# Five matmul operands at other SBUF addresses: 112, 96 and 160 modulo 256 bytes instead of 128

## The chip, the cores and the metric

The kernel runs on one core of one Trainium2 chip. The metric is the device time of one execution in microseconds (us); lower is better. One execution was also profiled. In its rows PE is TensorE's matmul side, PEld its weight loads, DVE VectorE, ACT ScalarE, POOL GpSimd and SP SyncE.

## The reference: what is computed

Two transformer-like blocks are applied to 512 tokens of width 1024 (the first block also carries 16 meta tokens). All arithmetic is float32.

```python
# first block: token mixer (S5 state space + mLSTM), then a convolved, gated feed-forward
h = concatenate([meta, x])                                  # 528 x 1024
proj = rmsnorm(h, g_pre) @ w_in ; ... ; x + rmsnorm(merged @ w_out, g_post)
a = causal_dwconv(h @ w_gate, w_conv, b_conv)               # 1024 -> 2816
y = (gelu(a) * (h @ w_up)) @ w_down                         # 2816 -> 1024
# second block: 16 attention heads of three kinds, then an MLP
proj = rms_norm(x, norm_g) @ w_in                           # q, k, v, gates
y = concatenate([y_moba, y_fox, y_dil]) @ w_out ; x = x + y
x + square(relu(rms_norm(x, norm_g) @ w_up)) @ w_down       # 1024 -> 4096 -> 1024
```

## The kernel before, in words

Activations lie transposed in SBUF: features on the 128 partitions, tokens along the free axis. The weights come in "units" of 128 x 1024 floats through a ring of four buffers (`w_raw`). ScalarE rounds a unit to `w_hi` (type fp32r) and VectorE makes the rest, `w_lo`. Each activation operand is kept as such a pair too, `..._hi` and `..._lo`. A product is three matmuls, hi by hi, lo by hi and hi by lo, for each of 8 blocks of 128 input features, all into one PSUM accumulation: 24 matmuls for one unit over 512 tokens. The helper `unit` (its matmul is L1939) does this; in a row `ps<-h_lo,w_hi` the first name is the moving operand, which streams through the array, the second the stationary one, which a weight load (LDWEIGHTS, PEld) puts there. Every matmul has its own weight load.

Moving operands are 512 tokens wide, or are cut in two halves of 256 and 260 (or 264 and 264) tokens where 516 or 528 tokens have to be covered, since a PSUM bank holds 512 floats.

Everything in SBUF has a hand-made address. `at(name, shape, where)` puts a tile at byte `where` of each partition, over others that are dead by then; the base names are `HX` (byte 82560), `Zu` (151488) and `R` (170176). In this document a *phase* is the byte address at which an operand's read begins, modulo 256. The tiles that matter, with their phases as the program has them before the change:

- `h2_hi`, `h2_lo` (shown as `h_hi`, `h_lo` in rows): input of every projection of the second block, 512 wide, row stride 2048 bytes: phase 128.
- `f_hi`, `f_lo`: input of the first block's feed-forward. The view begins 4 words into rows of 576 words (2304 bytes, nine times 256). The gate units (`ffn_gate`) read halves of 256 and 260 columns from column 0: phase 112 for both. The up units (`ffn_up`) read 512 columns from column 4: phase 128.
- `ffn_hi`, `ffn_lo`: the feed-forward's activations, moving operand of its down products: phase 128.
- `mlp_hi`, `mlp_lo`: the same of the second block's MLP: phase 128.
- `y_dil_hi`, `y_dil_lo` (72 matmuls) phase 128, and `w_hi`, `w_lo`, whose 128-column blocks all begin at phase 128: not touched by the change.
- In the first block `h_hi`, `h_lo` have rows of 528 words (2112 bytes), so the phase moves by 64 from one of the 8 feature blocks to the next. Units with halves of 264 begin at 128 + 64k and 160 + 64k, which over the 8 blocks are all the multiples of 32; units with halves of 256 and 260 (read from token 12) begin at 176 + 64k, that is 176, 240, 48 and 112.

Order is by hand: each engine's program is written out, and semaphores join them. TensorE waits in `begin` for the unit's `w_lo` and for the PSUM bank to be free.

Of the kernel before, what the change touches and what calls it, by code (L numbers as in the profile page):

```python
# [25 lines left out]
KT = D_MODEL // P  # L26
SEQ, META = 512, 16
# [3 lines left out]
TW = T1 - T0  # L31
# [124 lines left out]
def build(nc, w_units, x_t, cols_in, consts_in, sel_in, ssm_b_in, ssm_c_in, alibi_in, dil_in, out):  # L156
    fp32, f32r = mybir.dt.float32, mybir.dt.float32r
# [10 lines left out]
    def region(size):  # L168
        at = place[0]
        place[0] += size  # L170
        return at

    def at(name, shape, where, dt=fp32):
        return nc.alloc_sbuf_tensor_at(name, [P] + shape, dt, offset=where)
# [6 lines left out]
    HX = place[0]  # L181
# [12 lines left out]
    Zu = region(4 * T1 * 4)  # L194
# [41 lines left out]
    yahi = at("ya_hi", [CT, T1], R + 20 * T1 * 4, f32r)  # L236
    yalo = at("ya_lo", [CT, T1], R + 24 * T1 * 4, f32r)

    fhi = at("f_hi", [KT, 576], HX + (96 - HX) % 256, f32r)[:, :, 4:4 + TW]
    flo = at("f_lo", [KT, 576], Zu + (96 - Zu) % 256, f32r)[:, :, 4:4 + TW]  # L240
    RA = R + (128 - R) % 256
    fahi = at("ffn_hi", [KT, SEQ], RA, f32r)
    falo = at("ffn_lo", [KT, SEQ], RA + 16384, f32r)
    sq0 = [at(f"first_sq{j}", [T1], Zu + 2112 * j) for j in range(4)] + [sq[0], sq[1], rows, rs]
    sqp = [at(f"tile_sq{j}", [T1], R + 2112 * j) for j in range(KT)]
    gp = [at(f"gate_pad{j}", [T1 + 2], R + 256 + 32768 + 2144 * j) for j in range(2)]
# [1 line left out]
    tup = [at(f"up{j}", [SEQ], R + 256 + 41152 + 2048 * j) for j in range(2)]  # L248
    ctmp = at("conv_tmp", [SEQ], R + 256 + 45312)

    h2hi = at("h2_hi", [KT, SEQ], HX, f32r)
    h2lo = at("h2_lo", [KT, SEQ], HX + 4 * KT * SEQ, f32r)
    V = at("v2_tok", [4, D_MODEL], R)
    sgf = at("fox_gate", [3, SEQ], R + 16384)
    qa = [at(f"q_pair{j}", [SEQ], R + 22528 + 2048 * j) for j in range(2)]
# [16 lines left out]
    wf = at("w_forget", [KT * 32], Zv + 9216)  # L272
    dilr = at("dil_mask_r", [SEQ], Zv + 1024, f32r)

    mahi = at("mlp_hi", [KT, SEQ], RA, f32r)
    malo = at("mlp_lo", [KT, SEQ], RA + 16384, f32r)
    sqm = [at(f"mlp_sq{j}", [SEQ], Z2 + 2048 * j) for j in range(KT)]
    rl = [at(f"relu{j}", [SEQ], R + 33024 + 2048 * j) for j in range(2)]
    r2 = [at(f"relu_sq{j}", [SEQ], R + 37120 + 2048 * j) for j in range(2)]
# [2410 lines left out]
```

How the kernel before makes its waits and increments, by code:

```python
    def fence(self):  # L131
        if self.last is not None:
            self.eng.wait_ge(*self.last)
# [208 lines left out]
        @block.sync  # L343
# [12 lines left out]
            def load(s, r, j):  # L356
                sp.wait_ge(lo_ready, r + (s - RING + 1))
                sp.dma_start(raw[:, j, :], w_units[bass.ds(r + s, 1), :, :].rearrange("a p c -> p (a c)")
                             if not isinstance(r, int) else w_units[r + s]).then_inc(raw_in[j], 16)
            trips = (UNITS - RING) // RING
            with sp.Fori(0, trips) as i:
                for j in range(RING):
                    load(RING + j, i * RING, j)
            for n in range(RING + trips * RING, UNITS):
                load(n, 0, n % RING)
            for m in range(KT - 1):
                sp.wait_ge(sem("out_ready"), m + 1)
                sp.dma_start(out[:, m * SEQ:(m + 1) * SEQ], ot[m % 2][:, :]).then_inc(sem(f"out_done{m % 2}"), 16)
            for hf in range(2):
                sp.wait_ge(sem("out_ready"), KT + hf)
                c0 = hf * SEQ // 2
                sp.dma_start(out[:, (KT - 1) * SEQ + c0:(KT - 1) * SEQ + c0 + SEQ // 2], ot[1][:, c0:c0 + SEQ // 2]
                             ).then_inc(sem("out_done1"), 16)
            sp.wait_ge(sem("out_done0"), 16 * KT // 2)
            sp.wait_ge(sem("out_done1"), 16 * (KT // 2 + 1))
# [16 lines left out]
            def post_square(norm, m, src):  # L394
                if m == 0:
                    act.wait_ge(sem("rs_ready"), norm)
                elif m >= 3:
```

## Time and profile before

| | |
|---|---|
| median of 3 runs | 1450.04 us (1449.85 to 1450.05) |
| the profiled execution's own time | 1451.67 us |
| its span, first to last instruction | 1449.9 us |
| TensorE matmul busy | 98% of the span, 9151 matmuls |
| granted TensorE clock | 0.999 of full speed |

The profiled execution's time is 1.8 us above its span and 1.6 us above the median. A matmul's record in the timeline has a start and a length; matmuls overlap, so the length says little about throughput. The distance from one start to the next, here called the *pitch*, is what a matmul costs in a running stream.

### The profile page before, as it was taken

How to read it: one execution, taken by the hardware profiler on the slowest of the kernel's cores; microseconds unless marked ns; L12 is line 12 of the kernel's file. 1: busy time of each engine (PE TensorE's matmuls, PEld its weight loads, DVE VectorE, ACT ScalarE, POOL GpSimd, SP SyncE). 2: the span in 40 equal slices, each digit the busy share in tenths (PEclk: the TensorE clock that was granted, in tenths of full speed). 3: DMA queues.
4: the chain of work that ended last, by engine and by line, in shares of the span. 5: the costliest groups of instructions: out<-in, count | busy, mean ns of one | idle time of the engine just before them, and what ended most of it. 6: DMA issues, size and time to landing. Idle time of an engine off the chain costs nothing.

```text
span 1449.9 us, 23195 instructions
## 1 busy us (share of the span) xinstructions
PE 1425.1 (98%) x9151; PEld 1229.5 (85%) x9151; DVE 844.1 (58%) x1267; ACT 606.9 (42%) x924; POOL 305.1 (21%) x287
## 2 busy tenths in 40 slices
PE   8999999999999999999999999999999999999999
PEld 7999999999998988998998777767678888888887
DVE  6888554457465543554355637898877534344355
ACT  6552577643343321222124445666645314233230
POOL 2660333300115621560364000002103000000000
PEclk9999999999999999999999999999999999999999
DMA  5212111223312322323233132101133323323321
GB/s 206 74 60 76 58 59 66 67 86 138 109 64 73 102 101 88 101 87 101 88 102 126 64 104 73 59 29 59 44 117 117 102 88 102 102 87 103 100 93 68
DMA packets 35846, 128.30 MB, mean 88 GB/s; under 512 B 4084, under 2 KB 4468, under 8 KB 35632
## 3 DMA queue, kind: packets, MB, share of 16 engines
q1 hardware_dynamic: 34608, 122.18, 25.5%
q10 hardware_dynamic: 864, 4.33, 0.8%
q8 instruction: 63, 1.03, 0.3%
q0 software_dynamic: 288, 0.57, 0.1%
q14 instruction: 23, 0.19, 0.0%
HBM read 124.92 MB, written 2.10 MB: 88 GB/s over the span
## 4 chain that ended last, share of the span: by engine, by line
PE 70%; DVE 11%; ACT 8%; POOL 7%; issue 2%; DMA 0%; ACTq 0%; DVEq 0%; SPq 0%; POOLq 0%
PE ps L1939 59%; PE ps L2345 3%; DVE w_lo L967 2%; POOL gate_conv L1757 2%; POOL conv_tmp L1860 2%; ACT w_hi L392 2%; DVE rot L971 2%; POOL phase_tmp L1757 1%; PE ps L2464 1%; PE ps L2441 1%; PE ps L2403 1%; ACT conv_tap L516 1%; DVE rot L1223 1%; POOL gate_conv L1857 1%; PE ps L2454 1%
## 5 line engine op out<-in xcount | busy, mean ns | idle before, releaser
L967 DVE TENSOR_TENSOR w_lo<-w_raw,w_hi 128x1024 fp32r<-128x1024 f32 (+2 forms) x225 | 294.1, 1309 | 168.1 <-ACT w_hi L392 167.1
L1939 PE MATMUL ps<-h_hi,w_hi 128*128 128x512 f32 (+3 forms) x1168 | 332.6, 334 | 5.1 <-DMA consts<-consts 2.2
L1939 PE MATMUL ps<-h_hi,w_lo 128*128 128x512 f32 (+3 forms) x1168 | 321.7, 325 | 0.0
L1939 PE MATMUL ps<-h_lo,w_hi 128*128 128x512 f32 (+3 forms) x1168 | 321.6, 324 | 0.0
L392 ACT ACTIVATE w_hi<-w_raw 128x1024 fp32r<-128x1024 f32 (+2 forms) x226 | 231.0, 1032 | 171.8 <-PE ps L1939 166.2
L1939 PEld LDWEIGHTS ps<-h_hi,w_hi 128*128 128x128 f32 x1168 | 196.8, 189 | 34.4 <-issue 11.7
L1939 PEld LDWEIGHTS ps<-h_lo,w_hi 128*128 128x128 f32 x1168 | 196.7, 189 | 19.7 <-issue 2.9
L1939 PEld LDWEIGHTS ps<-h_hi,w_lo 128*128 128x128 f32 x1168 | 196.4, 189 | 17.9
L1939 PE MATMUL ps<-f_hi,w_hi 128*128 128x256 f32 (+1 forms) x488 | 129.6, 319 | 0.0
L1939 PE MATMUL ps<-f_hi,w_lo 128*128 128x256 f32 (+1 forms) x488 | 129.6, 319 | 0.0
L1939 PE MATMUL ps<-f_lo,w_hi 128*128 128x256 f32 (+1 forms) x488 | 129.5, 319 | 0.0
L1939 PE MATMUL ps<-mlp_lo,w_hi 128*128 128x512 f32 (+1 forms) x264 | 101.1, 383 | 0.0
L1939 PE MATMUL ps<-mlp_hi,w_hi 128*128 128x512 f32 (+1 forms) x264 | 101.1, 383 | 0.0
L1939 PE MATMUL ps<-mlp_hi,w_lo 128*128 128x512 f32 (+1 forms) x264 | 101.1, 383 | 0.0
L1939 PEld LDWEIGHTS ps<-f_hi,w_hi 128*128 128x128 f32 x488 | 82.3, 188 | 7.9 <-DVE w_lo L967 0.4
L971 DVE TENSOR_TENSOR y_sum<-y_sum,ps 128x512 f32<-128x512 f32 (+2 forms) x40 | 27.0, 674 | 105.4 <-PE ps L1939 105.4
L1939 PEld LDWEIGHTS ps<-f_hi,w_lo 128*128 128x128 f32 x488 | 80.9, 188 | 6.7
L1939 PEld LDWEIGHTS ps<-f_lo,w_hi 128*128 128x128 f32 x488 | 80.9, 188 | 6.0
L1857 POOL TENSOR_SCALAR gate_conv<-gate_pad,cols 128x512 f32<-128x512 f32 x22 | 28.1, 1276 | 201.3 <-DVE gate_pad L971 201.3
L1939 PE MATMUL ps<-ffn_hi,w_hi 128*128 128x512 f32 (+1 forms) x170 | 65.6, 386 | 2.8 <-DVE ffn_lo L971 2.1
L1939 PE MATMUL ps<-ffn_lo,w_hi 128*128 128x512 f32 (+1 forms) x170 | 65.0, 382 | 0.0
L1939 PE MATMUL ps<-ffn_hi,w_lo 128*128 128x512 f32 (+1 forms) x170 | 64.9, 382 | 0.0
(381 smaller groups left out, 2235.6 us busy)
## 6 DMA issues: line engine op xcount, KB each, us to landing
w_raw<-w_units SPq DMA_DIRECT2D x227, 512.0 KB, 3.3
x<-x_t ACTq DMA_DIRECT2D x1, 2112.0 KB, 8.5
out<-out_tile SPq DMA_DIRECT2D x7, 256.0 KB, 2.0
x<-x_t ACTq DMA_DIRECT2D x3, 528.0 KB, 9.0
x<-x_t ACTq DMA_DIRECT2D x2, 264.0 KB, 4.5
consts<-consts SPq DMA_DIRECT2D x1, 320.0 KB, 6.7
b_step<-ssm_b SPq DMA_DIRECT2D x1, 256.0 KB, 10.3
c_step<-ssm_c SPq DMA_DIRECT2D x1, 256.0 KB, 11.0
```

The source lines that it names most:

```text
L392: A.do(dn.activation(whi[:, s % RING, 0:w], raw[:, s % RING, 0:w], ACT.Copy), hi_ready)
L516: A.do(dn.activation(tap[k % 3][:, 0:T1 - k], src[:, 0:T1 - k], ACT.Identity, scale=col("w_qk", 8 * (3 - k) + m)), sem("tap_ready"))
L967: Dv.do(v.tensor_tensor(wlo[:, s % RING, 0:w], raw[:, s % RING, 0:w], f32(whi[:, s % RING, 0:w]), ALU.subtract), lo_ready)
L971: Dv.do(v.tensor_tensor(o, a, b, op), s)
L1223: Dv.do(v.tensor_tensor_scan(w[:, g, :], decay, w[:, g, :], start, M, A_))
L1757: Po.do(g.tensor_tensor(o, a, b, op), s)
L1857: Po.do(g.tensor_scalar(dst[:, :], src[:, META:META + SEQ], w[0], w[3], M, A_))
L1860: Po.do(g.tensor_scalar(ctmp[:, :], src[:, META + k:META + k + SEQ], w[k], 0.0, M, A_))
L1939: ins = mm(o, wt[:, s % RING, w], xt[:, kx, c0:c0 + n], start=(b == 0 and a == 0), stop=(b == len(blocks) - 1 and a == 2))
L2345: ins = mm(PS[:, banks[t], :], xt[:, k, P * t:P * t + P], wt[:, s % RING, b * SEQ:b * SEQ + SEQ], start=(k == 0 and xt is h2hi and wt is w ...
L2403: mm(PS[:, qk_unit(i, w) % 2, :], blk64, sq[w][:, 0:SEQ], start=True, stop=True).then_inc(sem("qstat_mm"), 1)
L2441: ins = mm(PS[:, 2 + 3 * hh + bank, c:c + w], qa[i % 2][r, P * t:P * t + P], ka[i % 2][r, 0:w], start=False, stop=True, skip_group_check=T ...
```

## The change

Only start addresses change, by 16 or 32 bytes (and a gap between `h2_hi` and `h2_lo`). The instructions of all five engines, their order, their shapes and their semaphores are the same as before. A tile that isn't a multiple of 32 bytes away is made a little wider and read from word 4 on (`shifted`).

| moving operand | phase before | phase after |
|---|---|---|
| `h2_hi`, `h2_lo`, 512 wide | 128 | 112 |
| `f_hi`, `f_lo`, 512 wide (up units) | 128 | 112 |
| `f_hi`, `f_lo`, halves of 256 and 260 (gate units) | 112 | 96 |
| `ffn_hi`, `ffn_lo`, 512 wide | 128 | 160 |
| `mlp_hi`, `mlp_lo`, 512 wide | 128 | 96 |

In the value products of the second block (L2345) `h2_hi` and `h2_lo` are the stationary operand and the weights move; there the stationary's phase goes from 128 to 112.

```diff
-    fhi = at("f_hi", [KT, 576], HX + (96 - HX) % 256, f32r)[:, :, 4:4 + TW]
-    flo = at("f_lo", [KT, 576], Zu + (96 - Zu) % 256, f32r)[:, :, 4:4 + TW]
+    fhi = at("f_hi", [KT, 576], HX + (96 - HX) % 256, f32r)[:, :, 0:TW]
+    flo = at("f_lo", [KT, 576], Zu + (96 - Zu) % 256, f32r)[:, :, 0:TW]
     RA = R + (128 - R) % 256
-    fahi = at("ffn_hi", [KT, SEQ], RA, f32r)
-    falo = at("ffn_lo", [KT, SEQ], RA + 16384, f32r)
+    fahi = at("ffn_hi", [KT, SEQ], RA + 32, f32r)
+    falo = at("ffn_lo", [KT, SEQ], RA + 16416, f32r)
...
-    h2hi = at("h2_hi", [KT, SEQ], HX, f32r)
-    h2lo = at("h2_lo", [KT, SEQ], HX + 4 * KT * SEQ, f32r)
+
+    def shifted(name, where, words):
+        wide = at(name, [KT * SEQ + words], where, f32r)
+        return wide[:, words:words + KT * SEQ].rearrange("p (a b) -> p a b", a=KT)
+
+    H2 = HX + (96 - HX) % 256
+    h2hi = shifted("h2_hi", H2, 4)
+    h2lo = shifted("h2_lo", H2 + 4 * KT * SEQ + 256, 4)
...
-    mahi = at("mlp_hi", [KT, SEQ], RA, f32r)
-    malo = at("mlp_lo", [KT, SEQ], RA + 16384, f32r)
+    mahi = at("mlp_hi", [KT, SEQ], RA - 32, f32r)
+    malo = at("mlp_lo", [KT, SEQ], RA + 16352, f32r)
```

## Rows read from the trace of the kernel before

**Rows 1.** The page's busy time of each engine.

```profile
PE 1425.1 (98%) x9151; PEld 1229.5 (85%) x9151; DVE 844.1 (58%) x1267; ACT 606.9 (42%) x924; POOL 305.1 (21%) x287
```

**Rows 2.** Stretches: length, busy PE, PEld, DVE, ACT, POOL, granted clock, DMA share, GB/s.

```profile
445.00:795.00 350.00, 347.17 (x1992) 305.90 (x1992) 169.10 (x181) 98.89 (x120) 150.26 (x116) 1.00 0.30 99
900.00:1075.00 175.00, 171.74 (x929) 123.87 (x928) 147.84 (x278) 110.09 (x226) 17.67 (x13) 1.00 0.18 58
1100.00:1447.00 347.00, 346.73 (x1551) 287.62 (x1549) 160.01 (x182) 102.13 (x128) 12.18 (x7) 1.00 0.29 95
```

**Rows 3.** The longest piece of the chain that ended last: start us, us.

```profile
1125.42 321.32 PE ps L1939 x1440
```

**Rows 4.** Matmuls by shape, with their count; hi by hi of each operand.

```profile
L1939 PE MATMUL ps<-h_hi,w_hi 128*128 128x512 f32 x448 | 180.9, 404 | 0.4 <-DVE h_lo L980 0.3
L1939 PE MATMUL ps<-mlp_hi,w_hi 128*128 128x512 f32 x248 | 96.5, 389 | 0.0
L1939 PE MATMUL ps<-f_hi,w_hi 128*128 128x512 f32 x168 | 65.7, 391 | 0.0
L1939 PE MATMUL ps<-ffn_hi,w_hi 128*128 128x512 f32 x158 | 61.8, 391 | 2.8 <-DVE ffn_lo L971 2.1 <-DVE y_sum L971 0.7
L1939 PE MATMUL ps<-f_hi,w_hi 128*128 128x260 f32 x160 | 45.3, 283 | 0.0
L2345 PE MATMUL ps<-w_hi,h_hi 128*128 128x512 f32 x64 | 25.3, 395 | 0.4 <-ACT h_hi L740 0.4
```

**Rows 5.** Timeline, PE, 512 wide at phase 128: start us, length us.

```profile
1229.79 0.39 PE L1939 MATMUL ps<-mlp_hi,w_lo 128*128 128x512 f32 x1
...
1239.99 0.39 PE L1939 MATMUL ps<-mlp_hi,w_lo 128*128 128x512 f32 x1
```

**Rows 6.** Timeline, PE, the last unit: 256 wide at phase 128.

```profile
1440.82 0.28 PE L1939 MATMUL ps<-mlp_hi,w_hi 128*128 128x256 f32 x1
...
1446.45 0.28 PE L1939 MATMUL ps<-mlp_hi,w_lo 128*128 128x256 f32 x1
```

**Rows 7.** Timeline, PE, a gate unit: 256 and 260 wide at phase 112.

```profile
574.32 0.40 PE L1939 MATMUL ps<-f_hi,w_hi 128*128 128x256 f32 x2
...
579.76 0.40 PE L1939 MATMUL ps<-f_hi,w_lo 128*128 128x256 f32 x2
```

**Rows 8.** Timeline, PE, first block: 256 and 260 wide at phases 48, 112, 176, 240.

```profile
377.12 0.40 PE L1939 MATMUL ps<-h_hi,w_hi 128*128 128x256 f32 x2
...
382.60 0.40 PE L1939 MATMUL ps<-h_hi,w_lo 128*128 128x256 f32 x2
```

**Rows 9.** Timeline, PE, first block: 264 wide at the multiples of 32.

```profile
130.55 0.41 PE L1939 MATMUL ps<-h_hi,w_hi 128*128 128x264 f32 x2
...
135.94 0.41 PE L1939 MATMUL ps<-h_lo,w_hi 128*128 128x264 f32 x2
```

**Rows 10.** Timeline, PE, the up unit behind the gate unit of rows 7.

```profile
579.99 0.39 PE L1939 MATMUL ps<-f_hi,w_hi 128*128 128x512 f32 x1
...
581.38 0.39 PE L1939 MATMUL ps<-f_hi,w_hi 128*128 128x512 f32 x1
...
585.24 0.39 PE L1939 MATMUL ps<-f_hi,w_lo 128*128 128x512 f32 x1
```

**Rows 11.** Timeline, PE, records of plain float32 matmuls: three of a run, then four.

```profile
877.93 1.45 PE L2403 MATMUL ps<-sq,consts 128*128 128x512 f32 x3
...
877.93 1.88 PE L2403 MATMUL ps<-sq,consts 128*128 128x512 f32 x4
```

**Rows 12.** Timeline, PE and PEld: a matmul and the weight load beside it.

```profile
1300.06 0.39 PE L1939 MATMUL ps<-h_hi,w_hi 128*128 128x512 f32 x1
1300.07 0.19 PEld L1939 LDWEIGHTS ps<-h_lo,w_hi 128*128 128x128 f32 x1
```

**Rows 13.** Waits: who waited for whom, us in total, times, longest.

```profile
ACT w_hi L392 <- PE ps L1939: 166.2, 40, 6.5
```

## The prediction

> **What bounds the kernel now.** I read the page first. TensorE is busy with matmuls for 98% of the span, the other engines for 58% or less [rows 1]. In the stretches where the changed operands are read, PE idles 2.8 of 350 us (feed-forward of the first block), 3.3 of 175 us (attention) and 0.3 of 347 us (MLP), at a granted clock of 1.00, the 2.4 GHz level [rows 2]. The chain that ended last says the same: its longest piece is 321.32 us of PE alone [rows 3]. ScalarE, which makes the weights ready, waits 166.2 us for TensorE to give ring buffers back, not the other way round [rows 13]. So the time of the changed matmuls is on the path nearly one for one, and the question is what one of them costs.
>
> **The pitch, and how it depends on phase.** A busy share of 98% doesn't say that PE is at its peak. From one start to the next, 45 matmuls of 512 columns at phase 128 take 1239.99 - 1229.79 = 10.20 us, 226.7 ns each [rows 5]. At 2.4 GHz 512 columns are 213.3 ns. So 13.4 ns, 32 cycles, go to something else. At 256 columns and the same phase it is the same amount: 47 starts in 5.63 us are 119.8 ns, and 256 columns are 106.7 ns, so 13.1 ns [rows 6]. It is not a price of issuing a matmul: with plain float32 operands one more record adds 1.88 - 1.45 = 0.43 us [rows 11], and two passes over 512 columns (the page has twice as many such records as the program has matmuls) are 426.7 ns, so hardly anything is added there. What differs is how fast the operand is read. A weight load of 128 columns starts with each matmul [rows 12] and reads SBUF too. Thirty-two cycles is 128 floats in pieces of 16 bytes. That the load and the stream disturb each other where they begin at the same phase is my reading; no row proves it.
>
> Rows at other phases, all taken to 256 columns by subtracting extra columns at 1/2.4 ns each:
>
> - phase 112, halves of 256 and 260: 23 pairs in 579.76 - 574.32 = 5.44 us, 236.5 a pair, 118.3 a matmul, less 0.8 is 117.4 ns [rows 7];
> - phases 48, 112, 176, 240 mixed: 23 pairs in 5.48 us, 119.1, less 0.8 is 118.3 ns [rows 8];
> - all multiples of 32 mixed, 264 wide: 22 pairs in 5.39 us, 122.5, less 3.3 is 119.2 ns [rows 9];
> - phase 128: 119.8 ns [rows 6].
>
> So phase 128 is the dearest of the four, and 112 the cheapest, by 2.4 ns. A confounder stays: the last unit's matmuls go one after another into one bank, the halves alternate between two.
>
> The Trainium skill speaks against any effect. Advanced Engine Details and Errata, Memory Cachelines, has 16-byte lines in SBUF, with full performance as long as a line is hit at least twice; all of 96, 112, 128 and 160 are multiples of 16 and the reads are contiguous, so by that rule the price would be the same and the sum zero. TensorE: Matmul & The Clock Gate, Back-to-back issue gap, gives 518 cycles for 512 columns, 215.8 ns; the trace disagrees with 226.7 ns. An estimate by that page, were every changed matmul to reach its gap, is 3126 times 10.9 ns, 34 us less. Neither page is used in the sum.
>
> **The change part by part.** Nothing is added, removed or reordered; only phases change. Counts are three times those of hi by hi [rows 4], with a few blocks from other lines of code added.
>
> 1. 512 wide, 128 to 112: `h2` 3 x 448 = 1344, `f` 3 x 168 + 24 (first units, other lines) = 528; together 1872. No row has 512 columns at 112. Bounds: 0 (the 512-wide stream keeps its 226.7), and the full difference at 256 columns, 119.8 - 117.4 = 2.4 ns. I take 2.4, since the extra is the same 13 ns at either width [rows 5, 6]: -4.5 us.
> 2. 512 wide, 128 to 96 (`mlp`, 3 x 248 = 744) and to 160 (`ffn`, 3 x 158 + 36 = 510): 1254. Both phases are multiples of 32; the nearest row gives 119.8 - 119.2 = 0.6 ns, the other mix 1.5 ns [rows 6, 8, 9]. I take the middle, 1.0 ns: -1.3 us. The 84 half-width ones of the last units move with them, under 0.1 us.
> 3. Gate halves, 112 to 96: 6 x 160 = 960 and 96 in the first units, 1056. They leave the cheapest phase. Against 117.4 ns the two mixes are 0.9 and 1.8 ns dearer [rows 7, 8, 9]; I take 1.4: +1.5 us. Bounds 0 and 2.4 ns, +2.5 us.
> 4. Value products, 3 x 64 = 192, whose stationary goes to 112 while the moving weights stay at 128 [rows 4]: they too leave the state of equal phases. No row shows it; 2.4 ns either way is 0.5 us. I take 0.
> 5. Writes of the same tiles by ScalarE and VectorE: they lie under TensorE's work in rows 2 (DVE busy 160 of 347 us in the MLP stretch). I take 0. Without that cover a slower write would count once a unit.
>
> Sum: -4.5 - 1.3 + 1.5 = -4.3 us. In the attention stretch a little is lost to waits for softmax work that don't shrink; PE is 98% busy there [rows 2], so I leave 0.1. That is 1451.67 - 4.2 = 1447.5 us for an execution like the profiled one, which stands 1.6 us above the median; for the median 1445.8.
>
> **The rivals.**
>
> - *No effect.* The pitch of a 512-wide matmul is a fixed 226.7 ns, and what rows 7 to 9 show comes from halves alternating between two banks. Then items 1 and 2 are nothing and only item 3 counts, 0 to +2.5 us: 1450 to 1452.5. For it: the extra is constant over width, and at phase 128 settles exactly at 32 cycles. Against it: the phase mixes differ among themselves, 117.4, 118.3 and 119.2, though all alternate. The line rule of the Trainium skill named above (Advanced Engine Details and Errata, Memory Cachelines) would also give this case.
> - *Much faster.* If equal phases are what costs 32 cycles, another phase may free most of them for a wide stream, which unlike a half streams on for long after the load. The bound is 213.3 ns plus the 1 ns or so of rows 11: 12 ns x 3126 = -38 us, 1412. Half of the extra gone, 6.7 ns, is -21 us, 1429. Against it: at 112 the halves keep some 10.7 of 13 ns.
> - *Slower.* At equal phases the stream settles. It needn't elsewhere: behind a gate unit the first six 512-wide matmuls take 581.38 - 579.99 = 1.39 us, 231.7 ns each, and the next 17 take 3.86 us, 227.1 ns [rows 10]. A pitch above 226.7 exists, then, when load and stream are out of step. If at 112 they stay out of step, item 1 turns into 1872 x 5.0 = +9.4 us, and with item 3 the time is about 1461. It decides from about +2 ns per matmul of item 1 on. If it is only one of the two new phase groups, 1254 x 5.0 = +6.3, 1454 to 1456. For it: six rows of the trace per up unit. Against it: these are transitional, and the steady rows off 128 are cheaper, none dearer.
>
> **How the numbers follow.** Forecast mechanism (a few ns for each off 128) 0.43, no effect 0.25, much faster 0.12, slower 0.20. A measurement of this kernel tells about 0.2% (2.9 us) from no change. Of the forecast's 0.43 some 0.05 lies within 0.2% of before; of no effect all but 0.02 on the fast side. So faster 0.52, same 0.28, slower 0.20. The prediction is that of the forecast mechanism, 1445.8. Its own range is 1442 (items 1 and 2 all at 2.4 ns, -7.5 us, item 3 at nothing, and the 5 ns of excess of the first six matmuls of some 20 up units gone, -0.6 us) to 1449. The whole range has to reach into the neighbours: down to 1434, which leaves out most of the much faster case, up to 1455, which leaves out the worse half of the slower one.
>
> **What would show it.** In the timeline after: 512-wide matmuls of `h` and `f` with a pitch near 224.3 ns, of `mlp` and `ffn` near 225.7, gate halves near 119.7 instead of 118.3. A MLP piece of the chain shorter than 321.32 us. Durations of ScalarE and VectorE unchanged. The prediction is wrong if the 512-wide pitches at 112 are still 226.7, or above, or under 221, and if idle time of PE grows where I said that it bounds.

## The result, and the profile after

The changed kernel takes 1468.06 us (median of 4 runs, 1467.92 to 1468.13), the kernel before 1450.04 us (median of 4). The ratio is 1.0124, 95% interval 1.0109 to 1.0139: 18 us slower. Predicted were 1445.8 us, a range of 1434 to 1455, and a chance of 0.52 for faster. Direction and range are both wrong. The profiled execution took 1468.11 us with a span of 1466.3, against 1451.67 and 1449.9 before, so the spans differ by 16.4 us.

Page of the changed kernel, busy time of each engine (to be set beside [rows 1]):

```profile
PE 1445.2 (99%) x9151; PEld 1230.7 (84%) x9151; DVE 843.8 (58%) x1267; ACT 606.9 (41%) x924; POOL 304.9 (21%) x287
```

TensorE has 20.1 us more of busy time over the same 9151 matmul records. Weight loads, VectorE, ScalarE and GpSimd are what they were. PE's idle time fell from 1449.9 - 1425.1 = 24.8 us to 21.1, so 3.7 us came back and 16.4 are left.

The stretches of [rows 2] in the changed kernel: length, then busy PE, PEld, DVE, ACT, POOL, granted clock, DMA share, GB/s. Their ends are moved with the work.

```profile
445.00:799.00 354.00, 353.08 (x1991) 305.85 (x1990) 167.75 (x179) 97.77 (x119) 150.60 (x116) 1.00 0.30 98
906.00:1083.00 177.00, 174.25 (x929) 124.77 (x928) 147.45 (x275) 109.26 (x226) 17.64 (x13) 1.00 0.18 60
1108.00:1464.00 356.00, 355.17 (x1544) 286.46 (x1542) 158.51 (x181) 100.60 (x126) 10.99 (x7) 1.00 0.27 93
```

The granted clock is still 1.00, the 2.4 GHz level, so the loss isn't a clock. The feed-forward idles 0.9 us where it idled 2.8: part of what PE waited for is now hidden under slower matmuls.

Pieces of the chain that ended last, changed kernel: start us, us, engine, output, line, count.

```profile
307.45 106.23 PE ps L1945 x894
...
523.00 125.14 PE ps L1945 x723
...
658.79 102.50 PE ps L1945 x579
...
1132.47 330.71 PE ps L1945 x1440
```

The last piece answers to [rows 3]: 330.71 us instead of 321.32, for the same 1440 matmuls. The 894 matmuls of the first block before the feed-forward, which the change doesn't touch, take 106.23 us in both kernels.

Timeline of PE, changed kernel: start us, length us. In order: `h` 512 wide at 112; `mlp` 512 wide at 96; a gate unit's halves at 96; the up unit behind it (`f` at 112); and the last unit, 256 wide at 96.

```profile
1119.79 0.40 PE L1945 MATMUL ps<-h_lo,w_hi 128*128 128x512 f32 x1
...
1127.95 0.40 PE L1945 MATMUL ps<-h_hi,w_hi 128*128 128x512 f32 x1
...
1159.61 0.40 PE L1945 MATMUL ps<-mlp_hi,w_lo 128*128 128x512 f32 x1
...
1169.88 0.40 PE L1945 MATMUL ps<-mlp_lo,w_hi 128*128 128x512 f32 x1
...
574.32 0.40 PE L1945 MATMUL ps<-f_hi,w_hi 128*128 128x256 f32 x2
...
579.80 0.40 PE L1945 MATMUL ps<-f_hi,w_lo 128*128 128x256 f32 x2
...
580.04 0.40 PE L1945 MATMUL ps<-f_hi,w_hi 128*128 128x512 f32 x1
...
581.44 0.40 PE L1945 MATMUL ps<-f_hi,w_hi 128*128 128x512 f32 x1
...
585.41 0.40 PE L1945 MATMUL ps<-f_hi,w_lo 128*128 128x512 f32 x1
...
1457.34 0.28 PE L1945 MATMUL ps<-mlp_hi,w_hi 128*128 128x256 f32 x1
...
1462.90 0.27 PE L1945 MATMUL ps<-mlp_hi,w_lo 128*128 128x256 f32 x1
```

Between the first two rows lie 35 starts in 8.16 us, 233.1 ns each; between the next two 44 in 10.27 us, 233.4. In [rows 5] it was 226.7 ns. In cycles of 2.4 GHz that is 560 instead of 544: 512 columns and 48, where it was 512 and 32. The gate unit's 23 pairs take 5.48 us, 119.1 ns a matmul against 118.3 [rows 7]. The up unit runs at 233.3 ns from its first six matmuls and at 23 in 5.37 us, 233.5, over the whole: the slow start of [rows 10] (231.7, then 227.1) has become the steady state. The last unit, 47 starts in 5.56 us, is faster: 118.3 ns against 119.8 [rows 6].

The same by group. The means are worked out over the distances from each start of a group to the next start in the trace, with the long breaks (some tens of ns and more) left out; so they can lie about 1 ns above the pitch of a steady stretch. For `h` after the change they give 234.3, where the steady stretch above has 233.1. From here on *d* is the phase of the moving operand less that of the stationary one. The stationary one is the weights at 128, except for the value products, where the weights move and `h` is stationary.

| group (matmuls) | d | pitch before, ns | after, ns | sum, us |
|---|---|---|---|---|
| `h`, 512 wide (1344) | 0 to -16 | 227.4 | 234.3 | +9.3 |
| `f`, 512 wide (528) | 0 to -16 | 227.9 | 233.4 | +2.9 |
| `mlp`, 512 wide (744) | 0 to -32 | 226.7 | 233.3 | +4.9 |
| `ffn`, 512 wide (510) | 0 to +32 | 226.8 | 233.3 | +3.3 |
| `f`, gate halves (1056) | -16 to -32 | 118.3 | 119.2 | +1.0 |
| last units, 256 wide (84) | to -32, +32 | 119.8 | 118.2, 116.8 | -0.2 |
| value products (192) | 0 to +16 | 227.7 | 227.2 | -0.1 |
| `y_dil`, 512 wide, not moved (72) | 0 | 227.1 | 227.0 | 0 |

The sum is 21.1 us, against 20.1 us more of busy PE. Groups by shape, changed kernel (busy, mean ns of one, idle before it), for a changed operand and the one that stayed:

```profile
L1945 PE MATMUL ps<-ffn_hi,w_hi 128*128 128x512 f32 x158 | 62.7, 397 | 0.9 <-DVE ffn_lo L977 0.6 <-DVE y_sum L977 0.3
...
L1945 PE MATMUL ps<-y_dil_hi,w_hi 128*128 128x512 f32 x24 | 9.4, 392 | 0.5 <-DVE y_dil_lo L986 0.5
```

The mean of one `ffn` matmul rose from 391 [rows 4] to 397 ns, and the wait for `ffn_lo` fell from 2.1 to 0.6 us. Waits of the changed kernel (us in total, times, longest):

```profile
ACT w_hi L398 <- PE ps L1945: 171.0, 40, 5.0
```

ScalarE waits 5 us longer for PE than in [rows 13]: nothing but PE became a bound.

### The profile page after: what moved, and what is told of

It is laid out like the page before. It is cut to its first block, busy times and chain, and to the rows that moved or that the text cites. A ratio compares the mean times of both kernels' runs of the same rounds, so it can differ in the third digit from the quotient of the medians.

```text
span 1466.3 us, 23195 instructions
## 1 busy us (share of the span) xinstructions
PE 1445.2 (99%) x9151; PEld 1230.7 (84%) x9151; DVE 843.8 (58%) x1267; ACT 606.9 (41%) x924; POOL 304.9 (21%) x287
## 4 chain that ended last, share of the span: by engine, by line
PE 75%; DVE 10%; ACT 8%; POOL 4%; issue 2%; DMA 0%; SPq 0%; DVEq 0%; ACTq 0%; POOLq 0%
PE ps L1945 63%; PE ps L2351 3%; DVE w_lo L973 2%; DVE rot L977 2%; POOL phase_tmp L1763 1%; PE ps L2470 1%; ACT w_hi L398 1%; PE ps L2447 1%; PE ps L2409 1%; ACT conv_tap L522 1%; DVE rot L1229 1%; PE ps L2460 1%; POOL conv_tmp L1866 1%; POOL gate_conv L1763 1%; PE ps L2004 1%
## 5 line engine op out<-in xcount | busy, mean ns | idle before, releaser
L398 ACT ACTIVATE w_hi<-w_raw 128x1024 fp32r<-128x1024 f32 (+2 forms) x226 | 231.1, 1032 | 176.7 <-PE ps L1945 171.0
```

The costliest lines, as they stand in the source:

```text
L398: A.do(dn.activation(whi[:, s % RING, 0:w], raw[:, s % RING, 0:w], ACT.Copy), hi_ready)
```

## The experiments

Pitches in the text are means over a group, as in the table. Theories have letters in the expectations, which say what each holds. In short: A, only the distance d counts, and 512-wide streams at d = 0 are the one cheap case; B, the absolute address of the streamed operand counts, and multiples of 64 or 128 are cheap; C, `mlp` moved alone to 96 keeps its pitch, since the loss has its root elsewhere, in the placement of `h`. Kernels said to have one run are measured once and profiled in that run.

### One group alone

```diff
-    mahi = at("mlp_hi", [KT, SEQ], RA, f32r)
-    malo = at("mlp_lo", [KT, SEQ], RA + 16384, f32r)
+    mahi = at("mlp_hi", [KT, SEQ], RA - 32, f32r)
+    malo = at("mlp_lo", [KT, SEQ], RA + 16352, f32r)
```

> The kernel before with one part of the change alone: mlp_hi and mlp_lo begin at phase 96 instead of 128. Theory A (what counts is that the moving operand and the weights beside it begin at the same phase) and theory B (what counts is where the moving operand itself begins) both expect the 744 matmuls of 512 columns to go from 226.7 to the 233.3 ns of the changed kernel's trace, +4.9 us, 1455 us, with all other pitches as before. Theory C (the loss has its root elsewhere, in the h tiles' shifted placement, and spreads) expects under 1.5 us.

Measured: 1455.4 us (5 runs) against 1450.2, ratio 1.0037 (1.0022 to 1.0052). `mlp` goes to 233.35 ns, each other group stays as before. Chain of this kernel:

```profile
1125.87 326.28 PE ps L1939 x1440
```

The piece is 4.96 us longer than in [rows 3]: 744 times 6.6 ns is 4.9. Phase 96 costs as much as phase 112, so C is out, and the loss of one group adds up by itself.

### Other phases of the streams, weights at 128

Four kernels put the operands at many distances, and move the tiles behind them where they need the room. This edit of the first stands for the others:

```diff
-    h2hi = at("h2_hi", [KT, SEQ], HX, f32r)
-    h2lo = at("h2_lo", [KT, SEQ], HX + 4 * KT * SEQ, f32r)
+    H2 = HX + (192 - HX) % 256
+    h2hi = at("h2_hi", [KT, SEQ], H2, f32r)
+    h2lo = at("h2_lo", [KT, SEQ], H2 + 4 * KT * SEQ, f32r)
```

> The kernel before with four phases in one program, weights still at 128: h of the second block at 192, the MLP's activations at 0, the feed-forward's at 64, f's 512-wide reads at 160 (its halves at 144). Theory A: all four are off the weights' 128, so all go to about 233 ns, some 3100 x 6.6 ns = +20 us, about 1470. Theory B, that multiples of 64 are good starts: h, mlp and ffn stay at 226.7 and only f's 528 lose, +3.5 us, about 1454. Theory B with multiples of 128: mlp alone stays, +16 us, 1466.

Measured: 1461.5 us (1 run) against 1450.2. `h` at 192 takes 229.15 ns, `mlp` at 0 232.4, `ffn` at 64 233.3, `f` at 160 233.1. Multiples of 64 and of 128 lose too: B, in this form, is out. A isn't right in its size either: it expected about 233 ns for all four and 1470 us, and `h` loses only 1.8 ns, the kernel 11.3 us.

> Distance d is the moving operand's phase minus the weights' phase (128). One program with d of +48 (h of the second block), +16 (mlp), -48 (ffn), +96 (f, 512 wide). So far 0 gave 226.7 ns, -16, -32, +32, -64 gave 233.3, +64 gave 229, -128 gave 232. Theory A1 (cheap only where the load runs level with the stream or just behind it: d from 0 to +16): mlp 226.7, the other three 233. Theory A2 (cheap for all positive distances up to half the period, +32 being an outlier): h, mlp and f under 230.

> As the run before, with d of +4 (h of the second block), +112 (mlp), +8 (ffn), -96 (f, 512 wide). Theory A1: h and ffn 226.7, mlp and f 233. If the equal phase had to be exact, h and ffn would be at 233 too.

> As before, with d of -4 (h of the second block), +80 (mlp), -80 (ffn), -112 (f, 512 wide). Theory A1: all at 233; if pieces of 16 bytes count and not the single byte, h at -4 could still be between 226.7 and 233. A value well under 226.7 anywhere would say that a better placement exists.

Measured, one run each: 1464.42, 1471.69 and 1461.6 us against 1450.14. In the second, with `h` at 132, timeline of PE:

```profile
879.75 0.40 PE L1945 MATMUL ps<-h_hi,w_lo 128*128 128x512 f32 x1
...
883.32 0.40 PE L1945 MATMUL ps<-h_hi,w_lo 128*128 128x512 f32 x1
```

15 starts in 3.57 us are 238.0 ns: four bytes off the weights' phase is the dearest place of all. Mean pitches of 512-wide matmuls from all kernels, by d:

| d | 0 | -4 | +4 | +8 | +16 | -16 | -32, +32 | -48 | +48 |
|---|---|---|---|---|---|---|---|---|---|
| ns | 226.7 | 230.6 | 237.8 | 232.7 | 231.7 | 233.4, 234.3 | 233.3 | 231.5 | 231.95 |

| d | -64 | +64 | -80 | +80 | -96 | +96 | -112 | +112 | -128 |
|---|---|---|---|---|---|---|---|---|---|
| ns | 233.3 | 229.15 | 232.2 | 231.1 | 234.1 | 233.2 | 232.6 | 231.1 | 232.4 |

Most d are measured with one operand here, and operands differ at equal d (at -48 `ffn` has 231.5 with weights at 128, and in a later kernel, with weights at 160, `h` has 233.9 and `f` 234.3), so the hills among the values off zero are not to be read too closely. Nothing is below d = 0, and no other d reaches it. Why modulo 256: `h2_hi` (byte 82560) and `mlp_hi` (byte 170368) begin at 128 and 384 modulo 512, while the blocks of the weights lie 512 bytes apart; both run at 226.7 to 227.4 ns, so 512 is too much. And d = -128 costs 232.4 ns, so 128 is too little.

Both finer theories of the sweep failed. The one that had d from 0 to +16 free expected 226.7 ns for `h` at +4, `ffn` at +8 and `mlp` at +16; they have 237.8, 232.7 and 231.7. The other had all positive distances under 230 ns; those at +48 and +96 have 231.95 and 233.2. The value products at d = +16 were free in the changed kernel. In those products the roles are turned, the weights stream and `h` is loaded; no run gave the reason, and with `h` at 192 (d = -64) they lose as well, 233.3 ns, and with `h` at 132 and 124 (d = -4 and +4) they have 232.4 and 231.6.

### Moving the weights: the distance or the address

Theory A says that the weights can be moved instead of the streams, with the same loss, and that both moved together lose nothing. In the first kernel the weights go to 160, and no 512-wide stream with them. The placement shifts by 32 bytes ahead of the weights (the first block's `h` goes along), `h2` is put back to 128, the others stay.

```diff
+    place[0] += 32
...
-    h2hi = at("h2_hi", [KT, SEQ], HX, f32r)
-    h2lo = at("h2_lo", [KT, SEQ], HX + 4 * KT * SEQ, f32r)
+    H2 = HX + (128 - HX) % 256
+    h2hi = at("h2_hi", [KT, SEQ], H2, f32r)
+    h2lo = at("h2_lo", [KT, SEQ], H2 + 4 * KT * SEQ, f32r)
```

> The kernel before with w_hi and w_lo, and the first block's h with them, moved by 32 bytes to phase 160, while h of the second block, f (512 wide), ffn, mlp stay at 128 as moving operands. Theory A: all 3126 changed pitches go to about 233 ns though no moving operand moved, about 1470 us. Theory B: they stay at 226.7, 1450 us.

Measured: 1468.68 us (4 runs), ratio 1.0127 (1.0109 to 1.0145), and each 512-wide group at 233.0 to 233.3 ns, `y_dil` and the value products too. Chain:

```profile
524.58 125.08 PE ps L1941 x723
...
1134.76 330.49 PE ps L1941 x1440
```

In the second kernel everything shifts: weights, `h2`, `f`, `mlp`, `ffn` and the rest at 160.

```diff
+    place[0] += 32
...
-    RA = R + (128 - R) % 256
+    RA = R + (160 - R) % 256
...
+    H2 = HX + (160 - HX) % 256
```

> The whole placement of the kernel before moved by 32 bytes: weights at 160 and every 512-wide moving operand at 160 too. Theory A: equal phases, 226.7 ns as before, 1450 us. Theory B: the starts are off 128 (and off every multiple of 64), about 233 ns, 1470 us, as in the changed kernel, where ffn at 160 shows 233.3.

Measured: 1450.39 us (10 runs), ratio 1.0002 (0.9992 to 1.0012). Chain, and timeline of `mlp` at phase 160:

```profile
522.93 122.77 PE ps L1941 x723
...
1124.08 321.32 PE ps L1941 x1440
```

```profile
1229.81 0.39 PE L1941 MATMUL ps<-mlp_hi,w_lo 128*128 128x512 f32 x1
...
1239.78 0.39 PE L1941 MATMUL ps<-mlp_lo,w_hi 128*128 128x512 f32 x1
```

44 starts in 9.97 us are 226.6 ns, and the piece of 1440 has the 321.32 us of [rows 3] to the hundredth. None of the 512-wide streams moved in the first kernel and it lost everything; all moved in the second and it lost nothing. So what is cheap is the equality of the two phases, at 128 and at 160 alike, and not an address: that part of A is shown. That the distance alone sets the price away from zero is not shown; the values at -48 above differ by 2 to 3 ns.

The same on top of the changed kernel: its weights go to 160, where only `ffn` has d = 0.

```diff
+    place[0] += 32
```

> The changed kernel with w_hi and w_lo moved to phase 160 and none of its changed operands touched. ffn at 160 is then level with the weights; h and f (112) are at d = -48, mlp (96) at -64, y_dil (128) at -32. Theory A: the 510 ffn matmuls come back from 233.3 to 226.8 ns, -3.3 us, y_dil's 72 rise to 233, +0.5 us, the others stay within 231 to 234 ns, so about 1465 us and not above 1468. Theory B (the moving operand's own address): 1468, ffn at 233.3.

Measured: 1466.03 us (4 runs), ratio to before 1.0107 (1.009 to 1.0124). `ffn` is back at 227.1 ns without having been touched, `y_dil`, level until now, goes to 233.1, and the value products, at d = +48, to 232.2; `h`, `f` and `mlp` stay dear (233.9, 234.3, 233.3). Chain:

```profile
523.04 123.87 PE ps L1946 x723
...
1129.99 331.11 PE ps L1946 x1440
```

The piece of the feed-forward, 723 matmuls, gives back 1.27 of its 125.14 us; the MLP's, which has no `ffn` in it, gives nothing (331.11 against 330.71).

### One operand of a pair

A unit goes hi by hi, lo by hi, hi by lo over and over. The next two ask whether a matmul pays by its own distance, or by that of the weights that are loaded beside it. First only `w_lo` to 160:

```diff
+    place[0] += 32
```

(here between `w_hi` and `w_lo`, with `h2` back at 128).

> The kernel before with w_lo alone moved from phase 128 to 160 (moving operands stay at 128). Of the three matmuls of a block (hi by hi, lo by hi, hi by lo) only the last has w_lo as its stationary operand. Theory A with the load beside the stream (the weights of the next matmul are loaded while this one streams): the lo by hi matmul, beside which w_lo is loaded, goes from 226.7 to 233, the other two stay, about +7 us. Theory A by own weights: the hi by lo matmul goes to 233, the others stay.

Measured: 1467.73 us (1 run) against 1450.14. By kind, `mlp` has 232.9 ns (hi by hi), 239.0 (lo by hi, beside which `w_lo` is loaded) and 228.1 (hi by lo). Timeline of PE:

```profile
1249.75 0.40 PE L1941 MATMUL ps<-mlp_hi,w_hi 128*128 128x512 f32 x1
1249.99 0.40 PE L1941 MATMUL ps<-mlp_lo,w_hi 128*128 128x512 f32 x1
1250.22 0.39 PE L1941 MATMUL ps<-mlp_hi,w_lo 128*128 128x512 f32 x1
1250.45 0.40 PE L1941 MATMUL ps<-mlp_hi,w_hi 128*128 128x512 f32 x1
...
1253.25 0.40 PE L1941 MATMUL ps<-mlp_hi,w_hi 128*128 128x512 f32 x1
```

From first to last lie 15 starts, 3.50 us, 233.3 ns: the full loss per matmul, for one load in three. The dearest of the three is the one beside the moved load; the size is more than either theory expected, and `h` and `ffn` show the same order (`ffn` 232.0, 238.7, 229.0).

Then one of each pair of streams: `h_lo` and `mlp_hi` at 96, `ffn` whole.

```diff
-    h2lo = at("h2_lo", [KT, SEQ], HX + 4 * KT * SEQ, f32r)
+    h2lo = at("h2_lo", [KT, SEQ], HX + 4 * KT * SEQ + 224, f32r)
...
-    mahi = at("mlp_hi", [KT, SEQ], RA, f32r)
+    mahi = at("mlp_hi", [KT, SEQ], RA - 32, f32r)
```

> The kernel before with one of each pair moved to phase 96: h2_lo (its hi stays at 128), mlp_hi (its lo stays), and both of ffn as a yardstick; weights at 128. Theory A (each stream against the weights of the next matmul, matmul by matmul): the moved streams cost 233 ns and the unmoved 226.7, so h averages 228.9 (one moved of three) and mlp 231.1 (two of three). Rival, after the run with w_lo moved alone, where the three averaged 233.3: one operand out of step puts the whole sequence out of step, and h and mlp average 233.3 like ffn.

Measured: 1464.56 us (1 run) against 1450.14. `mlp`, two of whose three matmuls are off level, has 234.8, 231.1 and 233.9 ns, a mean of 233.3, as if all were. `h`, with one of three off level, has 228.4, 233.2 and 232.1, a mean of 231.2. Neither expectation holds for `h`: matmul by matmul it would have been 228.9, with the whole sequence out of step 233.3. But a matmul at d = 0 pays as well when its neighbours are off (231.1 in `mlp`, 232.1 in `h`), so the loss falls on the sequence and not on the single matmul.

### Is it the load's share of the reads?

If a weight load took reads from the stream, fewer columns loaded would cost less. This kernel leaves work out: in the first quarter of the MLP the loads take 96 of 128 columns, in the second and third 64, in the last 32, and the matmuls so many rows of output. `h` is at 96, `mlp` at 128.

```diff
-                    w = slice(kw * P, kw * P + P)
+                    w = slice(kw * P, kw * P + wc)
...
-                wide(U_MLP + 6 * KT + f)
+                wide(U_MLP + 6 * KT + f, wc=32)
```

> Leaves work out: in the MLP the weight loads (and so the output rows) are 96 columns wide in the first quarter, 64 in the second and third, 32 in the last, instead of 128; streams stay 512 wide. The up units read h at phase 96 (d = -32), the down units mlp at 128 (d = 0). Theory L (the extra cycles over 512 are the weight load's reads taken from the stream): the extra shrinks with the load, at d = 0 from 32 cycles (226.7 ns) to 24, 16, 8 (223.3, 220.0, 216.7 ns), at d = -32 from 48 cycles (233.3) to 36, 24, 12 (228.3, 223.3, 218.3). Rival (the extra belongs to the stream alone, from where it begins): 226.7 and 233.3 throughout.

Measured: 1462.34 us (1 run, with work left out). Timeline of PE at d = -32, loads of 96 columns, then of 32:

```profile
1135.74 0.39 PE L1940 MATMUL ps<-h_lo,w_hi 128*96 128x512 f32 x1
...
1137.34 0.39 PE L1940 MATMUL ps<-h_hi,w_lo 128*96 128x512 f32 x1
...
1394.82 0.41 PE L1940 MATMUL ps<-h_lo,w_hi 128*32 128x512 f32 x1
...
1407.78 0.41 PE L1940 MATMUL ps<-h_lo,w_hi 128*32 128x512 f32 x1
```

7 starts in 1.60 us are 228.6 ns, 54 in 12.96 us 240.0. With 128, 96, 64 and 32 columns the loads themselves take 188, 161, 134 and 108 ns, `h` has 233.3, 228.9, 231.7 and 239.7 ns, and `mlp` at d = 0 226.7, 230.0, 230.0 and 231.7. The theory of the load's reads expected 218.3 and 216.7 at 32 columns. Its one hit is `h` at 96 columns (228.3 expected); from there on the pitch rises while the load shrinks. So that reading is refuted, and so is the one in the prediction that 32 cycles are 128 floats in pieces of 16 bytes. The rival, pitches that don't depend on the load, is refuted as well. And equality of phases is no gain with every load: at 96 columns `mlp` at d = 0 is 1.1 ns slower than `h` at -32, though these are two operands.

### Does the width decide?

This kernel leaves work out too: the MLP streams 448, 384 and 320 of its 512 columns. `h` is at d = -32, `mlp` at 0.

```diff
-                wide(U_MLP + f, 0, sem("h4_lo") if f == 0 else None)
+                wide(U_MLP + f, 0, sem("h4_lo") if f == 0 else None, n=448)
...
-                    wide(U_MLP + 2 * KT + f, c * 16)
+                    wide(U_MLP + 2 * KT + f, c * 16, n=384)
```

> Leaves work out: in the MLP the streams are 448 columns wide in the first quarter, 384 in the second and third, 320 in the last, instead of 512; loads stay at 128 columns. Up units at d = -32, down units at d = 0. At 512 columns the extra is 48 and 32 cycles, at 256 it was 28 and 32. If the loss at d = -32 belongs to a long stream in proportion to its columns behind the load, the extra falls evenly from 48 to 28: 43, 38, 33 cycles (pitches 204.6, 175.8, 147.1 ns), at d = 0 32 cycles at every width (200.0, 173.3, 146.7 ns). Rival: a threshold, with 48 at 448 and 384 and a jump below.

Measured: 1376.04 us (1 run, with work left out). Timeline of PE, 384 wide at d = -32, then at d = 0:

```profile
1201.57 0.34 PE L1940 MATMUL ps<-h_hi,w_hi 128*128 128x384 f32 x1
...
1203.30 0.34 PE L1940 MATMUL ps<-h_lo,w_hi 128*128 128x384 f32 x1
...
1289.69 0.33 PE L1940 MATMUL ps<-mlp_lo,w_hi 128*128 128x384 f32 x1
...
1299.91 0.33 PE L1940 MATMUL ps<-mlp_hi,w_hi 128*128 128x384 f32 x1
```

The first two are 10 starts in 1.73 us, 173.0 ns, the others 59 in 10.22 us, 173.2.

| columns | pitch at d = -32, ns (cycles over) | at d = 0, ns (cycles over) |
|---|---|---|
| 512 | 233.3 (48) | 226.7 (32) |
| 448 | 204.5 (43) | 202.7 (38) |
| 384 | 173.4 (32) | 173.5 (32) |
| 320 | 146.6 (32) | 146.65 (32) |
| 256 | 118.2 (28) | 119.85 (32) |

The row of 512 at -32 is from the first experiment, that of 256 at -32 from the changed kernel. Both expectations missed. The extra doesn't fall evenly with the width (48, 43, 38, 33 cycles were expected; 384 columns have 32), and it doesn't stay at 48 down to a threshold either. Nor is it 32 cycles at every width at d = 0: 448 columns have 38. At 320 and 384 columns these two distances make no difference, at 448 and 512 the one off level is dearer. Two operands are compared here, `h` and `mlp`, so the 1.8 ns at 448 are weak by themselves; the 6.6 ns at 512 were measured on one operand.

At 256 columns d = -32 is 1.6 ns cheaper than d = 0, but that is no rule for other distances. The last units of the feed-forward in the second sweep kernel, at d = +8:

```profile
797.35 0.29 PE L1945 MATMUL ps<-ffn_lo,w_hi 128*128 128x256 f32 x1
...
799.75 0.28 PE L1945 MATMUL ps<-ffn_hi,w_lo 128*128 128x256 f32 x1
```

19 starts in 2.40 us are 126.3 ns. Over all kernels the last units lie between 113.5 (d = -64) and 123.5 ns (d = +8, a mean of this stretch and cheaper ones), the gate halves between 117.1 (d = +16) and 119.6 (d = +80).

## Why the prediction was wrong

- **What bounds the kernel**: right. The granted clock stayed 1.00, the wait of ScalarE grew with PE, and 20.1 us of PE's work became 16.4 us of span. Of the 3.7 us between the two, 1.9 are idle time of the feed-forward that the slower matmuls cover (2.8 to 0.9 us), which was not foreseen. Another 1.5 are in the start of the piece of 894 matmuls, at 307.45 instead of 308.93 in the chain of before; I read that as the profiled execution of before, which stands 1.6 us above its median, and not as the change: with the weights at 160, profiled in an execution 1.5 us above its median, the piece starts at 309.02. The medians, 18.0 us apart, are free of it: 20.1 - 1.9 = 18.2.
- **Item 1, the step that failed.** "I take 2.4, since the extra is the same 13 ns at either width" carried the gain seen at 256 and 260 columns [rows 6, 7] over to 512. At phase 128 the extra is indeed the same at both widths; its dependence on phase is not. At the new distances a 256-wide matmul gains (118.2 and 116.8 ns in the last units) and a 512-wide one loses. Forecast -4.5 us, measured +9.3 + 2.9 = +12.2 us. The table of widths shows it without another change.
- **Item 2** failed at the same step: forecast -1.3 us, measured +4.9 + 3.3 = +8.2 us. The experiment on `mlp` alone shows its 5 us by themselves. Its half-width matmuls gain 0.2 us, as the rows of 256 had said.
- **Item 3**, gate halves: right, +0.9 ns measured against +1.4 forecast, +1.0 us against +1.5, but with some luck: its reason, that 112 is the cheapest phase for the halves, doesn't hold (117.1 ns at 144, against 118.3).
- **Items 4 and 5**: right. The value products changed by -0.1 us. Writes of `mlp_lo` take 748 ns (761 before), of `h_lo` 746 (746), of `ffn_lo` 822 (821).
- **Phase as the variable.** The prediction spoke of phases of the moving operand, and called equality with the weights' phase the thing that costs 32 cycles. Equality is what saves 16, for a wide stream. The sentence "phase 128 is the dearest of the four" holds for 256 columns and those four rows alone. The confounder named there, banks that alternate, doesn't explain the rows away: the last unit writes to the same banks in both kernels and goes from 119.8 to 118.2 ns.
- **The rival that came true is the slower one**, with both its price and its reach too small. Its kind was right: a stream that doesn't settle, seen in the first six matmuls behind a gate unit [rows 10]. It was priced at 5.0 ns, from 231.7, and for item 1 or item 2. It is 6.6 ns for both (233.3 - 226.7), 3126 matmuls, 20.6 us. At its own 5.0 ns, but for both items, it would have given 1450 + 15.6 + 1.5 = 1467 us; the reach was the larger miss. It had been set at 0.20 because "the steady rows off 128 are cheaper, none dearer"; but all of these had at most 264 columns, and the only 512-wide rows off the settled state were the dear ones.
- **No effect** is refuted for the 512-wide ones. By the line rule of the Trainium skill, Advanced Engine Details and Errata, Memory Cachelines, as the prediction read it, it would have held; the trace disagrees, by 6.6 ns a matmul between starts that are all on a 16-byte line.
- **Much faster** is refuted over 18 distances.

What stays open is the mechanism inside. The runs show that it is between the stream and the weights, that between d = 0 and -32 it shows above 384 columns and not at 320 and 384, that it falls on whole sequences, and that it changes with the load's width, by no simple rule (128, 96, 64 and 32 columns: 6.6, -1.1, 1.7 and 8.0 ns between `h` at -32 and `mlp` at 0). They don't show what is out of step with what, why the steady states lie at 32 and 48 cycles, what sets the price at each distance off zero, or why the value products at d = +16 are spared. The Trainium skill, TensorE: Matmul & The Clock Gate, Step-by-step: what each phase is for, has two independent read ports for the stream and the weights. The kernel with the weights alone at 160 lost 18.5 us without a move of any 512-wide stream; whatever couples the two, it is not told by that sentence.

## What to carry to other kernels

Look at an operand's address beside that of the operand that is read together with it: here streams of 512 fp32r columns with loads of 128 columns want the same offset modulo 256 as their weights, and a placement may be shifted as a whole (1.0002) but not in parts (1.0124). Don't carry a pitch from one width to another: the same distance, -32, gained 1.6 ns at 256 columns and lost 6.6 at 512. And where a transient row (231.7 ns, six matmuls) is the only one of the wide shape off its settled state, it weighs more than many steady rows of another shape.

## What the runs showed of the hardware

- The steady pitch of a 512-wide fp32r matmul is 226.7 or about 233.3 ns, 544 or 560 cycles at a granted clock of 1.00, by whether it begins at the same byte modulo 256 as its weights; other distances gave 229.15 to 237.8, the last at four bytes.
- Weight loads of 32 columns instead of 128 raised the pitch from 233.3 to 239.7 ns at d = -32, and from 226.7 to 231.7 at d = 0; loads of 96 columns lowered it to 228.9 at d = -32 and raised it to 230.0 at d = 0.
- At 256 columns the dependence is another one: 119.8 ns at d = 0, 116.8 at +32, 113.5 at -64 (`mlp` of the kernel on top of the changed one), but 126.3 over 19 starts at +8. Two of the 113.5 are 227.0 ns, so halves at the best distance seen only equal one 512-wide matmul at d = 0. None of these runs beats the kernel before.
